# Moving the next tile's value projection, the end of the keys' norm and one turn inside the channel-tile loop of a diffusion block

## What is computed

```python
kk = kk / jnp.maximum(jnp.sqrt(jnp.sum(kk * kk, axis=-1, keepdims=True)), NORM_EPS)
...
def step(s, inp):
    w_t, k_t, v_t, kk_t, kka_t = inp[:5]
    sa = jnp.einsum('bhvk,bhk->bhv', s, kk_t)
    s = (s * w_t[:, :, None, :] - sa[..., None] * kka_t[:, :, None, :]
         + v_t[..., None] * k_t[:, :, None, :])
    y = jnp.einsum('bhvk,bhk->bhv', s, inp[5]) if len(inp) == 6 else None
    return s, y
```

## Time and profile before

| what | us |
|---|---|
| median of three runs | 1933.56 (1933.45 to 1933.71) |
| time of the profiled execution | 1936.53 |
| its span, first to last instruction | 1934.7 |
| loop over the eight tiles, from the trace | 135.7 to about 861 |
| one turn, tile 3 | 89.3 (408.16 to 497.42) |
| of it the sum part, and the state part | 57.6 and 31.6 |
| PE busy over the span | 1792.1 (93%) |
| DVE, ACT, POOL busy | 605.9, 433.2, 142.0 |

### The profile page before, as it was taken

One profiled execution on the slowest core, in us unless ns is written; L12 is line 12 of the kernel. 1 busy time (PEld: TensorE's weight loads), 2 busy tenths in 40 slices (PEclk: granted clock), 3 DMA queues, 4 the chain that ended last, 5 costly groups with the idle time before them and its releaser, 6 DMA issues.

```text
span 1934.7 us, 45703 instructions
## 1 busy us (share of the span) xinstructions
PE 1792.1 (93%) x20026; PEld 980.2 (51%) x20026; DVE 605.9 (31%) x1339; ACT 433.2 (22%) x724; POOL 142.0 (7%) x184
## 2 busy tenths in 40 slices
PE   5889999999999989785999999999999999999996
PEld 2356667676666767643434434434444344344342
DVE  3253647465564646425111111111111111111111
ACT  2214342424333333403011111111111111111111
POOL 0021203121212121200000000000000000000000
PEclk9989999999999999986699999999999999999998
DMA  9640212111111212006399999999999999999995
GB/s 369 249 193 25 71 36 60 47 61 46 50 57 40 67 29 78 4 1 272 157 403 422 422 421 422 422 421 422 422 422 422 422 422 422 422 422 422 422 422 214
DMA packets 75469, 489.72 MB, mean 253 GB/s; under 512 B 9632, under 2 KB 10704, under 8 KB 21440
## 3 DMA queue, kind: packets, MB, share of 16 engines
q1 hardware_dynamic: 75200, 487.46, 62.2%
q0 software_dynamic: 128, 0.11, 0.0%
HBM read 486.49 MB, written 1.05 MB: 252 GB/s over the span
## 4 chain that ended last, share of the span: by engine, by line
PE 51%; DVE 0%; ACT 0%; issue 0%; DVEq 0%; ACTq 0%
PE PS L1568 24%; PE PS L1614 12%; PE PS L1553 7%; PE PS L1560 3%; PE PS L1575 3%; PE PS L1600 1%; PE PS L1619 1%; DVE MT L1709 0%; DVE MT L1711 0%; ACT MT L1652 0%; DVEq L1515 0%; DVE y L1670 0%; ACT backT L1648 0%; DVE st L1708 0%; ACT y L1646 0%
## 5 line engine op out<-in xcount | busy, mean ns | idle before, releaser
L1568 PE MATMUL PS<-raw,hgT 128*64 128x512 f32 x2120 | 472.0, 598 | 0.0
L1568 PEld LDWEIGHTS PS<-raw,hgT 128*64 128x64 f32 x2120 | 147.5, 137 | 298.2 <-issue 298.2
L1614 PE MATMUL PS<-raw,actT 128*64 128x512 f32 x1056 | 232.2, 592 | 0.0
L732 PEld LDWEIGHTS PS<-raw 64*64 64x64 f32 x6912 | 156.0, 137 | 62.0 <-issue 51.9
L732 PE MATMUL PS<-raw 64*64 64x64 f32 x6912 | 171.7, 226 | 11.9 <-issue 5.4
L647 PE MATMUL PS<-arena 128*128 128x256 f32 x640 | 167.3, 400 | 10.4 <-ACT raw L444 10.4
L1683 DVE TENSOR_SCALAR back<-cst,now 128x128 f32<-128x128 f32 x66 | 19.9, 343 | 424.4 <-PE PS L1619 424.4
L1614 PEld LDWEIGHTS PS<-raw,actT 128*64 128x64 f32 x1056 | 75.9, 137 | 150.8 <-issue 150.8
L613 PE MATMUL PS<-arena 128*128 128x512 f32 x256 | 133.2, 645 | 16.6 <-DVE raw L1187 16.6
L1553 PEld LDWEIGHTS PS<-take,MT 128*128 128x128 f32 x1088 | 127.3, 196 | 30.9 <-issue 26.8
L1691 DVE TENSOR_SCALAR gate_half<-PS 128x512 f32<-128x512 f32 x33 | 22.8, 692 | 370.0 <-PE PS L1568 370.0
(11 more groups left out here) (300 smaller groups left out, 1780.6 us busy)
## 6 DMA issues: line engine op xcount, KB each, us to landing
raw<-in_w_exp SPq DMA_DIRECT2D x397, 1024.0 KB, 16.1
arena<-in_w_blk SPq DMA_DIRECT2D x67, 512.0 KB, 3.6
raw<-in_w_ada SPq DMA_DIRECT2D x24, 1024.0 KB, 9.9
arena<-in_w_out SPq DMA_DIRECT2D x8, 512.0 KB, 3.6
arena<-in_lora_up SPq DMA_DIRECT2D x8, 192.0 KB, 4.0
arena<-in_ctx SPq DMA_DIRECT2D x2, 512.0 KB, 5.7
xl<-in_x SPq DMA_DIRECT2D x2, 512.0 KB, 7.7
out_x<-MT SPq DMA_DIRECT2D x2, 512.0 KB, 3.1
```

The costliest lines, as they stand in the source:

```text
L732: ins = mm(out[H[h ^ to], c, :], lhsT[H[h ^ at], c, :], rhs[H[h ^ at], c, :], start=start, stop=stop)
L1568: ins = mm(PS[H[h], GU + g, :], hgT[:, s, :], raw[:, s, cols], start=False, stop=s == KT - 1, skip_group_check=True)
L1614: ins = mm(PS[H[m], Y, :], aT[:, q, H[h]], raw[:, KT + q, cols], start=q == 0 and h == 0, stop=q == 3 and h == 1, skip_group_check=True)
```

## The change

Five edits, all in `mixing`.

1. PE: the 16 products ahead are dealt out otherwise. Before: 3, 3, 2, 2, 1, 1, 2, 1, 1 behind `G2`, `G1n`, `Y2`, `Y4`, `N16P`, `Y8`, `Y16`, `ET`, `Y64`. After: 2, 2, 2, 2 behind `G2`, `G1n`, `Y2`, `Y4`, then 2, 2 behind `Y8` and `Y16`, 1 behind `vt`, 1 behind `X`, 2 behind `Y64`. Product 8, the first of the values, stands behind `Y8` now.
2. ACT and DVE follow: `mix` behind `Y4`, `square` behind `vt`, `norm` behind `BT`; the six steps of `keys` in three pairs behind the readout of `Y4` and the masks of `Y8` and `Y16`. `squares` stands behind `Y64` on PE.
3. DVE: only line 1058 of `norms` is left ahead of the state part. The two reciprocals and line 1064 are put at the head of the steps that `between` deals out, which are 31 with edit 4, and `between` takes three of them a time from step 4 on.
4. DVE: each scan of 512 tokens is two scans of 256.
5. PE: the turn `BT` is no stage of its own, but the `extra` of `Y64` (`flat`). It goes to bank 0, and the receptance projection waits for its copy.

```diff
@@ block.scalar, one turn
-                if j < KT - 1:
-                    square(j + 1)
...
-                if j < KT - 1:
-                    norm(j + 1)
...
-                act.wait_ge(S["BT_mm"], j + 1)
-                A(BT[0], bk("m", 1), ACT.Copy).then_inc(S["BT_ev"], 1)
+                if j < KT - 1:
+                    square(j + 1)
                 copy("ET", ET, "c", only=(0,))
                 copy("X", X, "n")
                 copy("Y64", YY, "m", only=(1,))
+                act.wait_ge(S["BT_mm"], j + 1)
+                A(BT[0], bk("c", 0), ACT.Copy).then_inc(S["BT_ev"], 1)
+                if j < KT - 1:
+                    norm(j + 1)
@@ block.tensor
+                def flat(c):
+                    for h in (0, 1):
+                        ins = mm(bk("c", 0)[H[h], c, :], BE[0][H[h], c, :], k("ident")[H[h], H[h]], start=True, stop=True)
+                    return ins
...
-                run(8, 10)
+                run(6, 8)
                 waits(1, "N8P_ev", "N8F_ev")
                 pair("N16P", "c", Q0F, Q0P, 0)
-                if j < KT - 1:
-                    squares(j + 1)
-                run(10, 11)
                 waits(1, "Y4_ev")
                 series("Y8", "m", Q0P, 0, keyed(0, "n"), "G30_mm")
-                run(11, 12)
+                run(8, 10)
                 waits(1, "N16P_ev", "Y8_ev")
                 series("Y16", "c", Q1P, 1, keyed(1, "m"), "G31_mm")
-                run(12, 14)
+                run(10, 12)
...
-                for c in range(NC):
-                    for h in (0, 1):
-                        ins = mm(bk("m", 1)[H[h], c, :], BE[0][H[h], c, :], k("ident")[H[h], H[h]], start=True, stop=True)
-                ins.then_inc(S["BT_mm"], 1)
+                run(12, 13)
...
-                waits(1, "ET_ev", "BT_ev")
-                series("Y64", "m", ET, 0)
-                run(15, 16)
+                waits(1, "ET_ev")
+                series("Y64", "m", ET, 0, flat, "BT_mm")
+                if j < KT - 1:
+                    squares(j + 1)
+                run(14, 16)
@@ block.vector
-                    step(nc.vector.tensor_tensor_scan(o, m, w, 0.0, ALU.mult, ALU.add), S["cum_dn"])
-                    yield
+                    for part in (slice(0, NTOK), slice(NTOK, T)):
...
+                        step(nc.vector.tensor_tensor_scan(op, mp, wp, 0.0, ALU.mult, ALU.add), S["cum_dn"] if part.start else None)
+                        yield
...
-                others = features(j + 1) if j < KT - 1 else iter(())
+                others = itertools.chain(normed, features(j + 1)) if j < KT - 1 else iter(())
...
-                        between(2)
+                        between(2 if i < 4 else 3)
```

More of the change, by code:

```diff
@@ L1 @@
+import itertools
 from contextlib import ExitStack, contextmanager
@@ L553, in _ @@
                 level("Y2", "N4F", Q1F)
+                copy("N8P", Q0P, "c")
+                level("Y4", "N8F", Q0F)
                 if j < KT - 1:
@@ L557, in _ @@
                     mix("k", k_sh, K_BANK, T, j + 1)
-                copy("N8P", Q0P, "c")
-                level("Y4", "N8F", Q0F)
-                if j < KT - 1:
-                    square(j + 1)
                 copy("N16P", Q1P, "c")
@@ L624, in receptance @@
                     pe.wait_ge(S["ET_ev"], 2 * j)
+                    pe.wait_ge(S["BT_ev"], 2 * j)
                 zblock(2, PS[:, R_BANK, 0:NTOK], NTOK, NTOK, S["z_mm"])
@@ L847, in _ @@
                     mean(j - 1)
-                run(0, 3)
+                run(0, 2)
                 pe.wait_ge(S["first_ev"], 4 * (j + 1))
@@ L858, in _ @@
                     var_and_bonus(j - 1)
-                run(3, 6)
+                run(2, 4)
                 waits(1, "N2P_ev", "N2F_ev")
@@ L867, in _ @@
                 level("Y2", Q0P, 1, 0, lambda c: readout(c, 0, one(EXTRAS)), "G40_mm")
-                run(6, 8)
+                run(4, 6)
                 waits(1, "N4P_ev", "N4F_ev")
@@ L902, in _ @@
                 ins.then_inc(S["ET_mm"], 1)
-                run(14, 15)
                 pe.wait_ge(S["vt_ev"], j + 1)
                 pair("X", "n", KF, [VT, VT], 0)
-                waits(1, "ET_ev", "BT_ev")
-                series("Y64", "m", ET, 0)
-                run(15, 16)
+                run(13, 14)
+                waits(1, "ET_ev")
[3 more added lines that the diff above has]
+                run(14, 16)
                 waits(1, "Y64_ev", "X_ev")
@@ L1076, in features @@
                     o, w, m = CUM[d], TW[d], k(f"scan{d}")
-                    if d == 1:
-                        o, w, m = o[:, ::-1], w[:, ::-1], m[:, ::-1]
-                    step(nc.vector.tensor_tensor_scan(o, m, w, 0.0, ALU.mult, ALU.add), S["cum_dn"])
-                    yield
+                    for part in (slice(0, NTOK), slice(NTOK, T)):
+                        op, wp, mp = o[:, part], w[:, part], m[:, part]
+                        if d == 1:
+                            op, wp, mp = op[:, ::-1], wp[:, ::-1], mp[:, ::-1]
+                        step(nc.vector.tensor_tensor_scan(op, mp, wp, 0.0, ALU.mult, ALU.add), S["cum_dn"] if part.start else None)
+                        yield
                 dve.wait_ge(S["omr_ev"], j + 1)
@@ L1192, in _ @@
                 readout(0, one(EXTRAS))
-                for _ in range(3):
-                    next(keyed, None)
                 level("Y4", "N8F", Q0F)
                 readout(1, one(EXTRAS))
+                for _ in range(2):
+                    next(keyed, None)
+                summed("Y8", "m")
+                triangle(0, "n")
+                for _ in range(2):
+                    next(keyed, None)
+                summed("Y16", "c")
+                triangle(1, "m")
+                for _ in range(2):
+                    next(keyed, None)
+                dve.wait_ge(S["TP_mm"], j + 1)
+                nc.vector.tensor_copy(TP[1], bk("n", 1)).then_inc(S["TP_ev"], 1)
                 for _ in keyed:
                     pass
[L1199 to L1206, removed]
                 dve.wait_ge(S["ET_mm"], j + 1)
                 ts(ET[1], bk("c", 1), -1.0, None, ALU.mult).then_inc(S["ET_ev"], 1)
-                next(normed, None)
                 dve.wait_ge(S["Y64_mm"], j + 1)
                 tt(YY[0], YY[0], bk("m", 0), ALU.subtract).then_inc(S["Y64_ev"], 1)
-                for _ in normed:
-                    pass
-                others = features(j + 1) if j < KT - 1 else iter(())
+                next(normed, None)
+                others = itertools.chain(normed, features(j + 1)) if j < KT - 1 else iter(())
                 def between(n):
```

## The result

| | before | after |
|---|---|---|
| median, us | 1933.71 (1933.45 to 1936.53, 5 runs) | 1921.08 (1918.68 to 1924.79, 5 runs) |
| ratio, 95% interval | | 0.9943 (0.9927 to 0.9958) |
| profiled execution | 1936.53 | 1920.57 |

By the medians the change takes 12.6 us off, by the ratio 11 (8 to 14); 16.6 were forecast. The median is 4 us above the number of the prediction and inside its range. The difference is in the main one term, part 4, which was 4.5 us too small; the others held within about 1 us each.

The account below looks back on a forecast made before the run. PE was taken to bound the loop, with the experts' stage behind it of fixed length. The terms -16.6 - 9.6 - 7.2 + 15.4 + 1.4 = -16.6 us took 1933.6 to 1917.0; 8-in-10 range 1907 to 1930.

Parts of the forecast that it names:

- part 4: State part: the norm's end and half scans put 4.5 us more on DVE; +2.2 us a turn, +15.4 us.
- What bounds the kernel: PE bounds the loop; the experts' weight stage has its own fixed length, so a microsecond off the loop shortens the result equally.
- Parts 1 and 2: Sum part, behind `Y4`: moving product 8 removes PE's wait, -16.6 us, and the half-rate clock stretches behind it, -9.6 us.
- The clock's rival: The half-rate stretch comes back in as many turns at another place: 1926.6 us; chance 0.13.
- the new waits that were watched in the sum part: Possible PE waits at `Y8`, `Y16`, `X` and `N2P`: none counted, 0.3 us a turn if the two tightest are missed.
- Part 3: Last sum: the turn, 0.98 us alone, costs 0.1 inside `Y64`; -0.9 x 8 = -7.2 us, bounds -7.8 and 0.
- The walk from hand-off to hand-off: State part: one turn's DVE deadlines followed step by step, giving +1.6 us a turn before POOL's contention.
- the choice of 0.6 between 0.4 and 1.4: State part: POOL beside DVE costs 0.4 to 1.4 us a turn; +2.2 taken from a range of +1.6 to +3.0.
- The sentence on the Trainium skill: State part: POOL slows DVE instructions with two SBUF inputs, not reciprocals; the upper bound, 21 us for 15.4, would be likelier.
- Part 5: Loop: one more "issue" wait of 0.7 to 0.8 us in one turn of four, +1.4 us, between 0 and 5.
- The cheap state part: State part: POOL misses line 1064 and three steps a time fit; +0.8 us a turn, 1907 us; chance 0.12.
- The slower one: State part: its new waits bring half-rate clock there, 22.4 us, with the state part's growth at 21: 1945 us; chance 0.07.

## Why the prediction was right, and where it was off

**What bounds the kernel.** Right. The loop is 12.4 us shorter and the medians 12.6, and from PE's last product of `y` to the end it takes 1072.3 to 1073.1 us in every kernel here, whatever its loop takes, but in the one with POOL's work left out: the experts' stage took none of it.

**Parts 1 and 2, the wait and the clock (-16.6 and -9.6).** Right in size. From the end of `Y4` to the start of `Y8` took 7.27 us in tile 3 before and 8.77 to 8.97 in the other six. With `squares` and one product taken off, which tile 3 sizes at 7.27 - 2.38 - 2.83 = 2.06, and with the 2.83 of now, the seven turns gain 26.3 us; 26.2 were forecast. Putting product 8 back brought wait and half rate back together (25.9 us). The clock's rival, that the half rate only moves, has fallen: no stretch between 137 and 785 us. That a wait of 2.4 us is not enough by itself stands too, with one turn in seven spared in each kernel, and not the same one; what tells that turn apart is open. Of the new waits that were watched in the sum part, none came at `X` or at `Y16`. The one at `N2P`, for ACT's copy of `AT`, came in two of seven turns, 0.41 and 0.31 us, 0.7 in all, where 0.3 a turn was allowed for it and `X` together.

**Part 3, the turn (-7.2).** Right: 0.93 us a turn by the sum parts, and 7.3 us by the ratios, with an error of some 4. The nearest row, `WT` and `U0` at 64 products in 2.10 us, was the right one.

**Part 4, the state part (+15.4).** This is the term that was mis-sized: +19.9 us, 2.84 a turn for 2.2. The walk from hand-off to hand-off held where DVE runs alone. Against where PE would have started, it started later by 0.45 (forecast 0.4) at step 1's `s`, 0.62 (0.5) at `u` of step 5, 0.27 (0.25) at step 6 and 1.11 (1.1) at step 7. But `u` of step 2 was 1.04 late where 0.4 stood in the walk, and step 2's `s` and step 3's `u` lost 0.14 and 0.29 where nothing stood. All three lie behind the instructions beside POOL. (The timeline's bracket counts from the end of the product ahead, which overlaps the next by about 0.1, so these are a little more than the brackets.) The walk alone gave +1.6 a turn, and taking POOL's work away brought 1.20 back: 1.6 + 1.2 = 2.8, the measured number. The step that failed is the choice of 0.6 between 0.4 and 1.4, "as the row with 0.43 and the one with 1.46 hold about as often". By its own bounds that was too low: with 0.4 at the least the range starts at 2.0 a turn, not at 1.6, and its middle is 2.5, 17.5 us. And a short instruction and a long one do not alternate by chance. The order of the program puts line 1069, line 1079 and two half scans beside POOL in every turn alike, and the upper bound was the nearer one: 1.24 over the walk's 1.6 was measured, against 1.4.

The sentence on the Trainium skill, "GPSIMD Engine Reference", section Specifications, stands up as far as it was used: with two SBUF inputs lines 1069 and 1086 take 979 and up to 995 ns for 752 and 692, and the reciprocal, of one input, takes 1753 beside POOL as without. By that rule the forecast would have been 21 us for this part, nearer to the 19.9 than the 15.4 taken.

**Part 5, "issue" (+1.4).** 12.5 us before and 14.9 after in tiles 0 to 6, +2.4: right in sign, a microsecond short. With the dealing of before it was 9.7. The two kernels with the large wait have 9.7 and 12.5, the eight without it 14.3 to 16.9. So a pause in front of PE's stream seems not to be wholly lost, and taking 26 us of them away gave 2 to 5 back; that the pause lets PE's stream run ahead is argued from these counts and not shown.

**The sum again.** In the sum parts of tiles 0 to 6, -26.3 for the wait and the clock, -6.5 for seven turns at 0.93 and +2.4 of "issue" make -30.4, for -30.5 measured. With +19.9 of the state parts and -1.8 of tile 7, whose half-rate stretches were shorter (6.8 us for 10.2), that is -12.3, for -12.4 in the loop.

**The rivals.** The cheap state part, +0.8 a turn, has fallen with the 2.84. The slower one too: the state part now has six waits of 0.2 to 1.0 us for DVE and one of 0.73 for ACT, 4.0 of 32 us in all, and not one stretch of half rate in seven turns. The rule of the Trainium skill that spoke for it, "TensorE: Matmul & The Clock Gate", section "A second HAM failure mode: psum-queue depth-cycling", did not apply to idles of this length here; no run here shows where it would.

What the prediction did not ask is whether part 4 belonged to the change at all. The earlier trace rows begin with the state part; the hole ahead of it, 7.92 us of idle DVE before and 9.31 after, was on the same timeline (tile 3). The other edits are worth 30 us together, and the norm's new place, with the three steps a time that it asks for, gave 18 of them back.

## What to carry to other kernels

Before work is moved on an engine, look for its idle stretch just ahead of the place: 4.3 us of DVE in a hole of 9 cost nothing, and behind the hole, between two hand-offs that PE waits for, they cost 0.77 us a turn, and 2.75 with the three steps a time that they brought. A step moved in among hand-offs is priced by walking the deadlines one after the other, with the durations that hold beside the other engine at work there, and not with those of a quiet one; these move with the moment at which the two meet (0.69 to 1.73 us for one half scan). And a wait for a PSUM bank's reader, in front of dense work, is worth its own length and more: removing 16.6 us of it brought 26.

## What was not expected of the hardware

**PE's "issue" waits come by the count of its instructions.** They stand inside dense trains of small products, in which nothing in the kernel holds PE. Two of the largest, tiles 1 and 3 of the changed kernel:

```profile
231.48 0.40 PE L734 MATMUL PS<-raw 64*64 64x64 f32 x12 [1.71 <-issue]
```

```profile
410.73 0.27 PE L734 MATMUL PS<-raw 64*64 64x64 f32 x2 [1.89 <-issue]
```

Counted along PE's stream (products, weight loads and the sequencer's own), all 22 of the loop before lie at the same place of every 256 instructions, and so do all 23 after. The page of the profile counts the instruction queue's packets:

```profile
q8 instruction: 121, 1.98, 0.4%
```

1.98 MB in 121 packets are 16.4 KB each. The Trainium skill, "Advanced Engine Details and Errata", section ISA Cache, gives a cache line of 16 KB, 256 instructions, with which both numbers agree. That the wait is for the next such line is argued from this agreement and not shown; no run here moves one on purpose. Each wait is 0.2 to 1.9 us, 0.8 on the mean (14.9 us in 18). The loop before has 114 such places, and 22 have a wait; there the 256 instructions ahead took 3.0 us at the median, and 5.1 at the places without one. That does not tell the two apart, since several stretches of 2.4 to 2.7 us have none.

**A one-column activation moves a table load.** The load of 1.28 us and its wait of 0.73 in each state part went with one instruction, 0.82 us a turn.

**DVE beside POOL.** A scalar operation of 128x512 takes 0.43 us alone and up to 0.89 beside POOL in the changed kernel (1.46 before), a half scan 0.69 and up to 1.00, 1.73 with the norm ahead, and a reciprocal is not touched.
